# A chunked delta net: the levels of a triangular inverse work on the half of the columns that each changes

## The reference, cut to what matters

```python
kk = jnp.einsum('bhnid,bhnjd->bhnij', k_beta, k) * decay
t_mat = jnp.where(strict, kk, 0.0) + jnp.eye(c, dtype=q.dtype)
u = lax.linalg.triangular_solve(t_mat, v * beta[..., None], left_side=True, lower=True, unit_diagonal=True)
w = lax.linalg.triangular_solve(t_mat, k_beta * jnp.exp(g)[..., None], left_side=True, lower=True, unit_diagonal=True)
...
v_new = u_n - jnp.einsum('bhck,bhkv->bhcv', w_n, state)
o_n = jnp.einsum('bhck,bhkv->bhcv', qd_n, state) + jnp.einsum('bhij,bhjv->bhiv', qk_n, v_new)
state = state * jnp.exp(gl_n)[..., None, None] + jnp.einsum('bhck,bhcv->bhkv', kt_n, v_new)
```

## Time and profile before

| what | value |
|---|---|
| median of 3 runs | 6801.14 us |
| lowest and highest run | 6796.91 and 6852.1 us |
| span of the profiled execution | 6812.4 us |
| mean granted TensorE clock of that execution | 0.840 of full speed |
| stage with the delta net, from its first DMA on | about 522.8 to 1062 us |

### The profile page before, as it was taken

The page is one execution under the profiler, slowest core; times in us unless marked ns, Lnnn a source line. Parts: engine busy times, 40 slices in busy tenths (PEclk is TensorE's granted clock), DMA queues, the critical chain, the costliest instruction groups (busy, mean ns, idle before and its releaser), DMA issues. The chain is left out here.

```text
span 6812.4 us, 88762 instructions
## 1 busy us (share of the span) xinstructions
PE 5198.9 (76%) x36228; PEld 3977.3 (58%) x36250; DVE 3153.4 (46%) x4036; ACT 1076.5 (16%) x1479; POOL 216.1 (3%) x157
## 2 busy tenths in 40 slices
PE   6797883399729898567577979768459976969988
PEld 4677882289707687234335858542435544758876
DVE  8435666544464575647474432325232345432233
ACT  3102222222212100310010210001111133111100
POOL 0000000011100000000000000003010000000000
PEclk8898996699858998568788889886558788989999
DMA  1221103511122353242323122233230012322233
GB/s 69 81 83 44 34 28 141 185 53 53 47 103 97 117 188 113 84 173 74 124 87 121 54 92 99 81 122 93 79 71 4 7 37 68 130 75 74 72 125 123
DMA packets 265766, 596.61 MB, mean 88 GB/s; under 512 B 27970, under 2 KB 126705, under 8 KB 264778
## 3 DMA queue, kind: packets, MB, share of 16 engines
q1 hardware_dynamic: 192614, 411.18, 18.2%
q10 hardware_dynamic: 55360, 120.08, 4.7%
q0 software_dynamic: 17536, 61.63, 2.6%
HBM read 400.61 MB, written 192.19 MB: 87 GB/s over the span
## 5 line engine op out<-in xcount | busy, mean ns | idle before, releaser
L386 PE MATMUL gu_ps<-kept_h_hi,gu_w_hi 128*128 128x512 f32 x704 | 275.0, 391 | 40.6 <-DVE gu_w_lo L119 40.6
L386 PE MATMUL gu_ps<-kept_h_lo,gu_w_hi 128*128 128x512 f32 x704 | 274.8, 390 | 0.0
L386 PE MATMUL gu_ps<-kept_h_hi,gu_w_lo 128*128 128x512 f32 x704 | 274.6, 390 | 0.0
L386 PE MATMUL win_ps<-kept_hn_hi,win_w_hi 128*128 128x512 f32 x576 | 224.9, 390 | 39.5 <-DVE win_w_lo L119 39.5
L3576 PE MATMUL be_ps<-be_hi,be_w_hi 128*128 128x512 f32 x512 | 202.9, 396 | 58.0 <-DVE be_lo L119 57.7
L386 PE MATMUL win_ps<-kept_hn_hi,win_w_lo 128*128 128x512 f32 x576 | 224.6, 390 | 0.0
L386 PE MATMUL win_ps<-kept_hn_lo,win_w_hi 128*128 128x512 f32 x576 | 224.6, 390 | 0.0
L3576 PE MATMUL be_ps<-be_lo,be_w_hi 128*128 128x512 f32 x512 | 200.6, 392 | 0.0
L3576 PE MATMUL be_ps<-be_hi,be_w_lo 128*128 128x512 f32 x512 | 200.6, 392 | 0.0
L2214 PE MATMUL lc_ps<-idft,lc_zz 128*128 128x256 f32 x512 | 121.0, 402 | 90.9 <-DVE lc_zz L2092 90.9
L421 DVE COPY win_o<-win_ps 128x1024 f32<-128x1024 f32 x36 | 44.1, 1225 | 285.5 <-PE win_ps L386 285.5
(11 more groups left out here) (678 smaller groups left out, 12647.1 us busy)
## 6 DMA issues: line engine op xcount, KB each, us to landing
rk_in<-s_decayed SPq DMA_DIRECT2D x8, 3072.0 KB, 16.0
oproj_mod_w<-in_ada_w POOLq DMA_DIRECT2D x12, 2048.0 KB, 9.3
gu_w<-in_w_gu SPq DMA_DIRECT2D x44, 512.0 KB, 3.3
win_w<-in_w_in SPq DMA_DIRECT2D x36, 512.0 KB, 3.3
s_z<-win_o ACTq DMA_DIRECT2D x36, 512.0 KB, 2.6
s_decayed<-rkp_ring SPq DMA_DIRECT2D x32, 512.0 KB, 2.8
dn_kv<-s_qkv SPq DMA_DIRECT2D x16, 768.0 KB, 6.0
oproj_w<-in_odd_w SPq DMA_DIRECT2D x24, 512.0 KB, 4.3
```

Of the source, the lines that this page charges most:

```text
L386: mm = pe.matmul(ps[:, u, h, :], a, b, start=(k == 0 and n == 0), stop=(k == kt - 1 and n == len(pairs) - 1))
```

## The change

The half of the columns that level l changes is picked by a strided view. With `s` = 2 and `e` = 2^l, `early` takes of each pair of blocks of 2^l columns the first in direction 0 and the second in direction 1; `late` takes the other one. Masking writes only the late columns of `off`, ACT copies only the early columns of `ys`, Y and the first Z product have 64 moving columns (early), the second Z product has 64 late ones, and the additions touch only those columns. The stationary operands (`off`, `xt`, `ys`) stay 128 columns wide. As the other columns of `off` and `ys` must be zero, each level has its own `off` and `ys` buffer. POOL clears these 26 tiles (7 + 6 per direction, 128x512 f32) once, at the start of the stage, and DVE waits for that ahead of its loop. The wait of the masks on earlier levels falls away.

```diff
-        self.at, self.x, self.xt, self.ys = (st.sb(n + s, [P, 4, P]) for n in ("at", "x", "xt", "ys"))
-        self.off = st.sb("off" + s, [P, 2, 4, P])
+        self.at, self.x, self.xt = (st.sb(n + s, [P, 4, P]) for n in ("at", "x", "xt"))
+        self.off = [st.sb(f"off{l}_{s}", [P, 4, P]) for l in range(levels)]
+        self.ys = [st.sb(f"ys{l}_{s}", [P, 4, P]) for l in range(1, levels)]
+    def early(self, t, l):
+        return t.rearrange("p h (b s e) -> p h s b e", s=2, e=1 << l)[:, :, self.d]
+    def late(self, t, l):
+        return t.rearrange("p h (b s e) -> p h s b e", s=2, e=1 << l)[:, :, 1 - self.d]
+    def clear(self, pool):
+        for t in self.off + self.ys:
+            pool.memset(t[:, :, :], 0.0).then_inc(self.zeroed, 1)
+    def wait_clear(self, eng):
+        eng.wait_ge(self.zeroed, 2 * self.levels - 1)
     def vector_off(self, dve, i, l, masks):
-        dve.wait_ge(self.y_done, i * self.levels + max(l - 1, 0))
-        if l == 2:
-            dve.wait_ge(self.x_ready, i * self.x_all + 2)
-        m = masks[:, l, :].unsqueeze(1).to_broadcast([P, 4, P])
-        dve.tensor_tensor(self.off[:, l % 2, :, :], self.at[:, :, :], m, ALU.mult).then_inc(self.off_ready, 1)
+        dve.wait_ge(self.y_done, i * self.levels)
+        m = masks[:, l, :].rearrange("p (b s e) -> p s b e", s=2, e=1 << l)[:, 1 - self.d]
+        shape = [P, 4, m.shape[1], m.shape[2]]
+        dve.tensor_tensor(self.late(self.off[l][:, :, :], l), self.late(self.at[:, :, :], l),
+                          m.unsqueeze(1).to_broadcast(shape), ALU.mult).then_inc(self.off_ready, 1)
...
         if l < self.levels - 1:
-            dve.tensor_tensor(self.x[:, :, :], self.x[:, :, :], dd[:, :, :], ALU.add).then_inc(self.x_ready, 1)
-        dve.tensor_tensor(self.xt[:, :, :], self.xt[:, :, :], a[:, :, :], ALU.add).then_inc(self.x_ready, 1)
+            x = self.early(self.x[:, :, :], l)
+            dve.tensor_tensor(x, x, self.early(dd[:, :, :], l), ALU.add).then_inc(self.x_ready, 1)
+        xt = self.late(self.xt[:, :, :], l)
+        dve.tensor_tensor(xt, xt, self.late(a[:, :, :], l), ALU.add).then_inc(self.x_ready, 1)
...
-        act.activation(self.ys[:, :, :], c[:, :, :], ACT.Copy).then_inc(self.y_copied, 1)
+        act.activation(self.early(self.ys[l - 1][:, :, :], l), self.early(c[:, :, :], l), ACT.Copy).then_inc(self.y_copied, 1)
...
-            mm = pe.matmul(c[:, h, :], self.off[:, l % 2, h, :], self.x[:, h, :] if l else ident,
-                           start=True, stop=True)
+            if l:
+                mm = pe.matmul(self.early(c[:, :, :], l)[:, h], self.off[l][:, h, :], self.early(self.x[:, :, :], l)[:, h],
+                               start=True, stop=True)
+            else:
+                mm = pe.matmul(c[:, h, :], self.off[0][:, h, :], ident, start=True, stop=True)
...
-                pe.matmul(dd[:, h, :], self.xt[:, h, :], self.ys[:, h, :], start=True, stop=True)
-            mm = pe.matmul(a[:, h, :], self.ys[:, h, :], self.xt[:, h, :], start=True, stop=True)
+                pe.matmul(self.early(dd[:, :, :], l)[:, h], self.xt[:, h, :], self.early(ys[:, :, :], l)[:, h],
+                          start=True, stop=True)
+            mm = pe.matmul(self.late(a[:, :, :], l)[:, h], ys[:, h, :], self.late(self.xt[:, :, :], l)[:, h],
+                           start=True, stop=True)
...
+            @block.gpsimd
+            def _(pool):
+                for d in range(2):
+                    inv[d].clear(pool)
...
                 dve.wait_ge(gate_c, 2)
+                for d in range(2):
+                    inv[d].wait_clear(dve)
                 with dve.Fori(0, NCH) as i:
```

More of the change, by code:

```diff
@@ L813, in __init__ @@
     def __init__(self, st, d, levels):
-        self.levels = levels
+        self.levels, self.d = levels, d
         s = f"{d}"
-        self.at, self.x, self.xt, self.ys = (st.sb(n + s, [P, 4, P]) for n in ("at", "x", "xt", "ys"))
-        self.off = st.sb("off" + s, [P, 2, 4, P])
-        self.off_ready, self.y_done, self.y_copied, self.z_done, self.x_ready = (
-            st.sem(n + s) for n in ("off_ready", "y_done", "y_copied", "z_done", "x_ready"))
-        self.x_all = 2 * levels - 1
-    def vector_off(self, dve, i, l, masks):
-        dve.wait_ge(self.y_done, i * self.levels + max(l - 1, 0))
-        if l == 2:
-            dve.wait_ge(self.x_ready, i * self.x_all + 2)
-        m = masks[:, l, :].unsqueeze(1).to_broadcast([P, 4, P])
-        dve.tensor_tensor(self.off[:, l % 2, :, :], self.at[:, :, :], m, ALU.mult).then_inc(self.off_ready, 1)
+        self.at, self.x, self.xt = (st.sb(n + s, [P, 4, P]) for n in ("at", "x", "xt"))
+        self.off = [st.sb(f"off{l}_{s}", [P, 4, P]) for l in range(levels)]
+        self.ys = [st.sb(f"ys{l}_{s}", [P, 4, P]) for l in range(1, levels)]
+        self.off_ready, self.y_done, self.y_copied, self.z_done, self.x_ready, self.zeroed = (
+            st.sem(n + s) for n in ("off_ready", "y_done", "y_copied", "z_done", "x_ready", "inv_zeroed"))
+        self.x_all = 2 * levels - 1
+    def early(self, t, l):
[7 more added lines that the diff above has]
+        eng.wait_ge(self.zeroed, 2 * self.levels - 1)
+    def vector_off(self, dve, i, l, masks):
+        dve.wait_ge(self.y_done, i * self.levels)
[3 more added lines that the diff above has]
+                          m.unsqueeze(1).to_broadcast(shape), ALU.mult).then_inc(self.off_ready, 1)
     def vector_x(self, dve, i, l, ident4, c, dd, a):
@@ L834, in vector_x @@
             dve.wait_ge(self.off_ready, i * self.levels + 1)
-            dve.tensor_tensor(self.xt[:, :, :], self.off[:, 0, :, :], ident4, ALU.add).then_inc(self.x_ready, 1)
+            dve.tensor_tensor(self.xt[:, :, :], self.off[0][:, :, :], ident4, ALU.add).then_inc(self.x_ready, 1)
             return
@@ L858, in tensor_z @@
         pe.wait_ge(self.y_copied, i * (self.levels - 1) + l)
+        ys = self.ys[l - 1]
         for h in range(4):
             if l < self.levels - 1:
-                pe.matmul(dd[:, h, :], self.xt[:, h, :], self.ys[:, h, :], start=True, stop=True)
-            mm = pe.matmul(a[:, h, :], self.ys[:, h, :], self.xt[:, h, :], start=True, stop=True)
+                pe.matmul(self.early(dd[:, :, :], l)[:, h], self.xt[:, h, :], self.early(ys[:, :, :], l)[:, h],
+                          start=True, stop=True)
+            mm = pe.matmul(self.late(a[:, :, :], l)[:, h], ys[:, h, :], self.late(self.xt[:, :, :], l)[:, h],
+                           start=True, stop=True)
         mm.then_inc(self.z_done, 1)
```

## The result

The changed kernel takes 6957.4 us (median of 4 runs, 6944.2 to 7008.4); the kernel before took 6800.3 us (median of 4). The ratio is 1.0225, 95% interval 1.0182 to 1.0268: slower, well beyond the noise; whether by more than 2% these runs leave open. The prediction said 6963 us. The profiled execution is the slowest of the four, with a span of 7006.6 us, 194.2 above that of before. 158 us of this difference lie where the change was made.

The account below looks back on a forecast made before the run. PE's passes were taken to bound the levels, with one short DVE wait each. Per chunk +21.7, +2.4 and -0.5 make +23.6 us; seven such chunks less 3.4 for one give +162, 6801 to 6963 us, range 6830 to 7035.

Parts of the forecast that it names:

- The pass has a floor: PE in the levels: halving columns saves nothing; a pass stays 0.112 us at 2.4 GHz, 0.214 at 1.2.
- Rival B: PE passes in the levels scale with their columns, 0.056 us each: 16.6 us less per chunk, 6668 us; chance 0.04.
- The clock stays at half speed until the full-width passes: PE stays at 1.2 GHz from level 0 to the state read behind level 6; levels' 272 passes take 58.2 us.
- +21.7: Added us per chunk from level 1's first pass to the state read: 58.2 in place of 36.5.
- How often: Of the 8 chunks, 7 lose the clock at 23.6 us each and one gains 3.4 us.
- Behind level 6 and ahead of level 1: Per chunk: slow full-width passes behind level 6 cost 2.4 us; shorter masks ahead of level 1 save 0.5.
- +2.4: Us per chunk for 16 to 32 full-width passes behind level 6 at 1.2 GHz; bounds 1.6 to 3.2.
- -0.5: Us per chunk saved ahead of level 1 by three half-length masks, part of it behind PE.
- The clearing: POOL's 26 memsets at the stage's start, before DVE's new wait: between 0 and +12 us once, taken as 0.
- The sum: Whole kernel: 7 x 23.6 - 3.4 = +162 us, from 6801 to 6963 us.
- Rival A: The clock stays or returns in level 1; half-width additions and masks save 3.4 us per chunk: 6774 us; chance 0.10.
- Rival C: Strided operands slow matmuls too, levels 1 and 2 at twice 0.214 us a pass: 7127 us; chance 0.04.

Follow-up runs that it names:

- e8: Changed kernel with only the 16 Y passes of level 1 back at 128 moving columns; 6780.6 us (one run).
- e1: Changed kernel with all matmuls of the levels back at 128 moving columns, all else as changed; 6782.6 us, 0.998 of the kernel before.
- e7: e5 plus 40 unread full-width identity passes per chunk in PE's gaps ahead of level 0's two groups; 6773.4 us, 0.9954 of the kernel before.
- e6: Changed kernel, narrow everywhere, plus 40 unread full-width identity passes per chunk ahead of level 0's two groups; 6804.7 us, 0.9991 of the kernel before.
- e3: Changed kernel with its narrow matmuls on 64 unbroken columns in place of strided ones, so no inverse is computed; 6974.5 us, 1.0271 of the kernel before.
- e2: Changed kernel with level 1's matmuls back at full width, levels 2 to 6 narrow; 6790.1 us, 0.9971 of the kernel before.
- e5: e1 with the clears shared out: POOL clears the 14 off tiles, ACT the 12 ys tiles; 6777.3 us, 0.996 of the kernel before.

## Why the prediction was right, step by step

**The pass has a floor** (shown). 0.112 us at 2.4 GHz and 0.214 at 1.2 were taken for 64 columns; the measured distances are 0.112 and 0.213. Rival B is out. That the weight load sets this floor, as the prediction says, isn't shown: no run changed the stationary width. The 60 cycles that the Trainium skill (TensorE: Matmul & The Clock Gate, section Back-to-back issue gap) gives for an isolated matmul of up to 64 columns aren't seen in these f32 passes, which have a 128-wide weight load each.

**The clock stays at half speed until the full-width passes** (shown by e8 and e1 against after). 272 x 0.214 = 58.2 us was said, 58.03 measured. "+21.7" is +21.6. With the 16 Y passes of level 1 alone at full width the clock came back in all eight chunks (e8), without them in one of eight: it was they that brought it back before. The rule of the Trainium skill (TensorE: Matmul & The Clock Gate, section Why this matters for your kernels) to keep the engine busy didn't help in the changed kernel, where PE was busy for 64.61 of 64.85 us at 0.50; with the gap filled with full-width passes it did, in all eight chunks of e7 and in seven of e6.

**How often.** Seven of eight was said, and seven it was, in e3's trace too. That was a guess with luck in it. The last chunk, which fetches nothing for a next one, got the clock back 1.8 us into its narrow Y passes, so these don't keep it down in every case. PE's work doesn't tell this chunk from the fifth: in both the clock fell at the start of the second group of level 0 (1.64 and 1.79 us ahead of level 1), and PE was busy for all of the 3.3 us behind it, with 7 full-width passes and then 8 or 9 narrow ones. In the last the clock then came back; in the fifth, where DMA moved data at the same time (a share of 0.18 against none), it stayed at 0.50. Why there and not in the others, and why e6 lost it in one chunk and e2 and e8 in none, isn't settled.

**Behind level 6 and ahead of level 1.** +2.4 was taken; from the read to the new values it is 3.33 us on the mean of the seven chunks for 1.92, and to the output 2.75 for 2.57: +1.6. Ahead, -0.5 was taken and -0.54 came (5.48 + 4.18 us from the products of k and q to level 1, for 5.75 + 4.45). A lossy chunk so costs 22.6 us, not 23.6.

**The clearing** is the term that was mis-sized: 0 was taken. It costs the 3.8 us by which level 1 of the first chunk comes later, plus the 0.54 that this chunk's masks save, 4.3 us. It is within the bounds of 0 to +12, but comes in another way than I looked for. I looked at DVE's new wait, 20 us later; the cost is in a DVE instruction that ran beside POOL's memsets. e5 shows it by taking POOL's clears away from it. The Trainium skill (SBUF — State Buffer, section SBUF: two separate sides) describes a port pair that VectorE and GpSimd share as an exclusive lock, held for an instruction. The traces agree that one blocks the other (5.30 us beside the memsets, 0.74 without them in e5); but the DVE instruction waited through some ten memsets, not one.

**The sum.** 3.8 at the start, 151 for the levels and 11 for the tails of seven chunks, -4.1 for the levels of the last chunk, and -3.8 for the part ahead of level 1 in the chunks from the second on: +158, as measured. The forecast's +162 had the tails 6 too high and the clearing 4 too low; the levels and the last chunk, each about 1 off, make the rest. So the total is nearer than its parts.

**Rival A as a mechanism** (shown by e1): with the clock back in level 1, 3.4 us per chunk were said for the half-width additions and masks, and 3.5 came (64.9 to 61.4). It was the right price for a case that the narrow passes themselves shut out. **Rival C** is out by e3; the sentence of the Trainium skill (SBUF — State Buffer, section Door 1: The DMA port swizzle) on non-contiguous PSUM access isn't borne out for runs of 2 to 64 f32 columns in passes at this floor.

## What to carry to other kernels

Before cutting the columns of a matmul, look for rows of the same form with fewer columns: where 1, 65 and 128 columns cost the same, as here, fewer save nothing. Then ask what the full-width passes did for the clock: when the granted clock falls ahead of a loop, see which passes lift it, and leave those at full width. Put clears on an engine that shares nothing with what is needed at once, or start them so that they end before it; and read a wait's cost at the instructions beside it, not only at the wait.

## What the runs showed that I had not expected

Passes whose results nobody reads made the changed kernel about 2.2% faster (6957.4 to 6804.7 us; by the ratios to the kernel before, 1.0225 to 0.9991). A single 8x1024 DVE instruction was held for 5.30 us by memsets on another engine. And the granted clock in a stage that no kernel here changed moved between executions, and its time with it, from about 436 to 488 us for the same work, more than most of the edits studied here were worth.
